# A hybrid attention, SSM and MoE trunk on one core: the layer-1 mixer in another order

## The chip, the cores and the metric

The kernel runs on one core of a Trainium2 chip. The time is the device time of one execution, in microseconds; the median of three runs is given. TensorE does the matmuls, VectorE (DVE) and ScalarE (ACT) the elementwise work, GpSimd (POOL) a little of it, and SyncE (SP) issues the loads of the weights from HBM.

## The reference

A trunk of two layers over 256 tokens of width 1024, all in float32. Layer 0 is sliding-window attention with cross attention to a memory, and a dense SwiGLU. Layer 1, whose first half this change is about, is an SSM mixer and a mixture of eight experts:

```python
z, xbc, dt_raw, xq = split(h @ w_in)                 # 2048, 3072, 32, 1024 columns
xbc = silu(causal_depthwise_conv(xbc, conv_w, conv_b))   # 4 taps
xs, bmat, cmat = split(xbc)                          # 2048, 512, 512
dt = softplus(dt_raw + dt_bias);  a = -exp(a_log)
y = ssd_chunked_scan(xs, dt, a, bmat, cmat)          # 2 chunks of 128, 4 groups of 8 heads of 64
y = y + xs * d_skip
y = rmsnorm(y * silu(z), g_norm)
cross = memory_cross_attention(xq, mem_k, mem_v)     # 4 heads of 256
x = x + concatenate([y, cross]) @ w_out              # (2048 + 1024) x 1024
...
def step(state, inp):                                # one chunk of the scan
    acum = cumsum(dtk * a);  decay = exp(acum[t] - acum[s]) for s <= t
    y_diag = (ck bk^T * decay) @ (xk * dtk)
    y_off = (ck @ state) * exp(acum)
    new_state = state * exp(acum[-1]) + bk^T @ (to_end * xk * dtk)
```

## The kernel before

The program is one instruction list per engine, written out by hand and ordered by semaphores; nothing is scheduled by a compiler. The weights stream through in units of 1 MB: 8 x 128 rows by 256 columns (kind "a") or 4 x 128 rows by 512 columns (kind "b"). A unit is loaded into one of three ring slots, ScalarE writes its high part (`whi`, three buffers, `split_hi`), VectorE the rest (`wlo`, two buffers, `split_lo`), and TensorE multiplies three pairs of high and low parts (`mm3`), so a product keeps about float32 precision. On both engines `ahead(n)` does the splits up to unit n at the place in the list where it stands. The high part of unit n waits until unit n-3 has been used, the low part until unit n-2 has been.

Products of the projections go to four PSUM banks in turn (`PB[f % 4]` for fill f); `drained` counts the banks emptied. Bank 4 and 5 hold scores or transposes, 6 and 7 the rest.

The layer-1 mixer goes through its parts in this order on TensorE (from L1507 on):

1. four units of cross-attention queries, then the scores of head 20 (the four heads are numbered 20 to 23);
2. the small dt unit, and four units of B and C, with transposes, scores and values of a head behind each;
3. eight units of x, each followed by the transposes of the x unit before (`x_transposes`);
4. the scan: eight steps, s = 0 to 7, over two chunks of four groups. A step multiplies B with C (L1560), makes the decay sums of 2 x 4 heads (L1570), the new state (L1577) or the output of the old one (L1582), and the diagonal part for 8 heads (L1589). ScalarE takes the exponential of the decay (L720), VectorE multiplies it by the masked product (L1076), GpSimd makes decay rows (L464), x times dt (L471) and two more products (L477, L481);
5. eight units of z, in two banks per pair, whose silu VectorE multiplies into y (L1098); ScalarE sums the squares;
6. rstd of y on GpSimd (L442 to L448), y scaled on VectorE (L860), 32 transposes in groups of four pairs with high and low part behind each (L1298, L533, L869);
7. twelve units of the output projection, six per 512 columns, y first and cross attention last, and the addition to x.

The causal conv of a unit (`for j in range(12)` on ScalarE and VectorE) copies the fill from PSUM into `ub`, which has three columns of zeros ahead (L687). For each of its two tiles VectorE multiplies by the last tap and adds the bias (L1048), adds the other three taps one after the other (L1052), and ScalarE applies silu (L696):

```python
ve.tensor_scalar(cv[:, k, :], u[:, CW - 1:], w[:, CW - 1:CW], ..., ALU.mult, ALU.add)
for tap in range(CW - 2, -1, -1):
    ve.scalar_tensor_tensor(out=cv[:, k, :], in0=u[:, tap:tap + S], scalar=w[:, tap:tap + 1], in1=cv[:, k, :], ...)
```

Of the kernel before, what the change touches and what calls it, by code (L numbers as in the profile page):

```python
# [21 lines left out]
P = 128  # L22
# [72 lines left out]
def weight_units(a):  # L95
# [64 lines left out]
def trunk(nc, a, out):  # L160
    units = weight_units(a)
    XQ0, K0, V0, OUT0, K1, FFN0 = 5, 9, 13, 17, 25, 29
    V1, L1, MOE = FFN0 + 3 * FC, FFN0 + 3 * FC + 4, len(units)

    ctx = ExitStack()
    with ctx:
# [11 lines left out]
        cat_hi, cat_lo = sb("cat_hi", [P, 24, S], F32R), sb("cat_lo", [P, 24, S], F32R)  # L178
# [39 lines left out]
        with ExitStack() as l1:  # L218
            with ExitStack() as conv:
                ub = sb("ub", [P, 2, 2, S + CW - 1], F32, conv)  # L220
                cv = sb("cv", [P, 2, S], F32, conv)
                xcT = sb("xcT", [P, 2, 2, S], F32, conv)
            with ExitStack() as scan:
                zs = sb("zs", [P, 2, 512], F32, scan)
# [3 lines left out]
            sb("pair_d", [P, 2600], F32, l1)  # L228
            dtx, dtu, dtr_, dtm, dt, dta = (sb(n, [P, NT, NH], F32, l1) for n in ("dtx", "dtu", "dtr", "dtm", "dt", "dta"))
            cbm = sb("cbm", [P, P], F32, l1)  # L230
            btok = sb("btok", [P, P], F32, l1)
            xdt = sb("xdt", [P, HPG, PH], F32, l1)
        with ExitStack() as moe:
# [10 lines left out]
        sb("pair_e", [P, 2 * 2 * S + NT * 2 * 192 + NT * D])  # L244
        Lm = actf[:, :, :].rearrange("p a (h t) -> p a h t", h=4)
# [24 lines left out]

        hankel = [c[:, 16:24, :] for c in (cat_hi, cat_lo)]
# [10 lines left out]
            dt_ready ln_chain dta_full eac_done u_zero conv_chain conv_done silu_conv xT_full xs_ready hi_ready lo_ready  # L282
# [3 lines left out]
            yd_full yo_full yo_done yy_done yg_done rt_chain rt_exp final""".split()  # L286
# [41 lines left out]
        TR_BEFORE = {R_H0: 0, R_MEM0: 4, R_MEM1: 8, R_F0: 12, R_H1: 16, R_Y: 20, R_F1: 28}  # L328
        XN_BEFORE = {R_H0: 0, R_MEM0: 2, R_F0: 4, R_H1: 6, R_Y: 8, R_F1: 10, R_FIN: 12}
# [3 lines left out]
        def square_at(r, t, n):  # L333

            if r in (R_H0, R_MEM0):
                return SQ_BEFORE[r] + t
            return SQ_BEFORE[r] + (2 * t + n if r in (R_H1, R_FIN) else 2 * n + t)

        fills, last_unit = {}, []
        for name, start, n, per in (("kv", 0, 1, 1), ("q", 1, 4, 1), ("xq0", XQ0, 4, 1), ("k0", K0, 4, 1), ("v0", V0, 4, 2),  # L340
                                    ("out0", OUT0 + 6, 4, 1), ("k1", K1, 4, 1), ("v1", V1, 4, 2), ("xq1", L1, 4, 1), ("dt", L1 + 4, 1, 1),
                                    ("bc", L1 + 5, 4, 1), ("x", L1 + 9, 8, 1), ("z", L1 + 17, 8, 2), ("out1", L1 + 25, 4, 6)):
# [145 lines left out]
        def _(ac):  # L488
# [180 lines left out]
            for j in range(4):  # L669
                xq_out("xq1", j)  # L670
# [1116 lines left out]
```

## Time and profile before

| | us |
|---|---|
| median of 3 runs | 1677.37 (1677.33 to 1680.08) |
| profiled execution, its time | 1680.51 |
| profiled execution, its span | 1678.7 |
| TensorE busy | 1561.9 (93%) |
| VectorE busy | 1122.6 (67%) |
| ScalarE busy | 951.7 (57%) |
| GpSimd busy | 64.2 (4%) |
| mean granted clock of TensorE | 0.959 |

The span runs from the first to the last instruction of the core. Busy time is the time in which an engine had an instruction under way. The granted clock is a share of the full speed: 1.00 is 2.4 GHz, 0.50 is 1.2 GHz. A busy share averages over stages that have different limits, so the rows below are cut by stage: the mixer of layer 1 runs from 460.4 to 807.2 us.

### The profile page before, as it was taken

The page shows a single profiled execution, that of the slowest core. Times are in us where ns is not written, and L with a number is a line of the kernel's source. Part 1 is how long each engine was busy: PE and PEld are TensorE (multiplying, and loading weights), DVE is VectorE, ACT ScalarE, POOL GpSimd, SP SyncE. Part 2 cuts the span into 40 slices and gives each one's busy share as a digit, 9 for nine tenths or more (in the row PEclk, how much of TensorE's full clock was granted, in tenths as well). Part 3 has the DMA queues.
Part 4 walks back from the last instruction along what each step waited for, and adds up shares of the span by engine and source line. Part 5 has one row for each costly group of instructions (what it writes and reads, how often), then busy time and mean ns, then how long its engine had stood idle before and what let it go on. Part 6 is the DMA issues. An engine that isn't in the chain of part 4 may idle for free.

```text
span 1678.7 us, 22515 instructions
## 1 busy us (share of the span) xinstructions
PE 1561.9 (93%) x8652; PEld 1357.4 (81%) x8652; DVE 1122.6 (67%) x997; ACT 951.7 (57%) x959; POOL 64.2 (4%) x85
## 2 busy tenths in 40 slices
PE   6999999999998768969599999999999999999996
PEld 6998899999897757858478788888888888888885
DVE  4455454444646655444498788797978978788885
ACT  5444453434546432433356777777677776777763
POOL 1000000000100026000000000000000000000000
PEclk9999999999999979979689999999999999999998
DMA  8433355656543420425479999999998999989992
GB/s 268 150 102 126 124 177 178 197 178 191 181 134 101 126 76 1 151 75 176 150 253 344 324 326 373 319 350 332 332 371 310 349 341 333 355 314 365 328 346 111
DMA packets 229602, 391.88 MB, mean 233 GB/s; under 512 B 7280, under 2 KB 82208, under 8 KB 229536
## 3 DMA queue, kind: packets, MB, share of 16 engines
q1 hardware_dynamic: 229536, 390.96, 67.2%
q8 instruction: 46, 0.75, 0.2%
q14 instruction: 20, 0.16, 0.0%
HBM read 389.86 MB, written 1.07 MB: 233 GB/s over the span
## 4 chain that ended last, share of the span: by engine, by line
PE 74%; DVE 8%; DMA 6%; issue 5%; ACT 5%; POOL 0%; SPq 0%; ACTq 0%; DVEq 0%; POOLq 0%
PE PB L1279 22%; PE PB L1280 21%; PE PB L1281 21%; DMA y<-in_moe_w_down 4%; DVE cv L1052 2%; ACT whi L496 1%; PE PB L1642 1%; DVE xn_lo L847 1%; PE PB L1619 1%; DMA ring<-in_moe_w_gate 1%; PE PB L1298 1%; PE PB L1570 1%; ACT whi L501 1%; ACT hT_hi L501 1%; PE PB L1361 1%
## 5 line engine op out<-in xcount | busy, mean ns | idle before, releaser
L1279 PE MATMUL PB<-whi,cat_hi 128*128 128x512 f32 (+1 forms) x1048 | 405.9, 387 | 14.4 <-DVE cat_lo L1229 11.5
L501 ACT ACTIVATE whi<-ring 128x2048 fp32r<-128x2048 f32 x168 | 321.0, 1916 | 142.6 <-PE PB L1281 118.2
L1281 PE MATMUL PB<-whi,cat_lo 128*128 128x512 f32 (+1 forms) x1048 | 399.1, 381 | 0.0
L841 DVE TENSOR_TENSOR wlo<-ring,whi 128x2048 fp32r<-128x2048 f32 (+1 forms) x103 | 234.1, 2273 | 205.4 <-PE PB L1281 171.4
L1280 PE MATMUL PB<-wlo,cat_hi 128*128 128x512 f32 (+1 forms) x824 | 309.0, 375 | 0.0
L847 DVE TENSOR_TENSOR wlo<-ring,whi 128x2048 fp32r<-128x2048 f32 x112 | 255.5, 2288 | 66.8 <-ACT whi L501 66.7
L1279 PEld LDWEIGHTS PB<-whi,cat_hi 128*128 128x128 f32 x1048 | 200.2, 191 | 51.5 <-DVE wlo L847 11.3
L1281 PEld LDWEIGHTS PB<-whi,cat_lo 128*128 128x128 f32 x1048 | 199.9, 191 | 37.7
L496 ACT ACTIVATE whi<-ring 128x2048 fp32r<-128x2048 f32 (+1 forms) x103 | 195.4, 1899 | 52.2 <-PE PB L1281 41.3
L1279 PE MATMUL PB<-hT_hi,whi 128*128 128x256 f32 x744 | 215.8, 290 | 2.7 <-DVE hT_lo L869 1.8
L1280 PE MATMUL PB<-hT_lo,whi 128*128 128x256 f32 x744 | 212.9, 286 | 0.0
L1281 PE MATMUL PB<-hT_hi,wlo 128*128 128x256 f32 x744 | 212.8, 286 | 0.0
L1280 PEld LDWEIGHTS PB<-wlo,cat_hi 128*128 128x128 f32 x824 | 156.4, 190 | 26.2
L1279 PEld LDWEIGHTS PB<-hT_hi,whi 128*128 128x128 f32 x744 | 145.6, 196 | 3.8 <-DVE hT_lo L869 2.2
L847 DVE TENSOR_TENSOR hT_lo<-ring,whi 128x2048 fp32r<-128x2048 f32 x56 | 128.2, 2288 | 28.9 <-ACT whi L501 28.9
L1280 PEld LDWEIGHTS PB<-hT_lo,whi 128*128 128x128 f32 x744 | 145.4, 195 | 0.5
L1281 PEld LDWEIGHTS PB<-hT_hi,wlo 128*128 128x128 f32 x744 | 145.1, 195 | 0.0
L847 DVE TENSOR_TENSOR elo<-y,hT_hi 128x2048 fp32r<-128x2048 f32 x56 | 128.2, 2289 | 16.5 <-ACT hT_hi L501 16.1
L501 ACT ACTIVATE hT_hi<-y 128x2048 fp32r<-128x2048 f32 x56 | 107.4, 1918 | 37.2 <-PE PB L1281 31.0
L847 DVE TENSOR_TENSOR xn_lo<-y,st_hi 128x2048 fp32r<-128x2048 f32 x40 | 91.5, 2288 | 10.9 <-ACT st_hi L501 10.9
L1280 PE MATMUL PB<-hT_lo,cat_hi 128*128 128x512 f32 x224 | 90.2, 403 | 0.0
L1279 PE MATMUL PB<-hT_hi,cat_hi 128*128 128x512 f32 x224 | 88.7, 396 | 0.0
(248 smaller groups left out, 2215.1 us busy)
## 6 DMA issues: line engine op xcount, KB each, us to landing
ring<-in_moe_w_gate SPq DMA_DIRECT2D x64, 1024.0 KB, 6.8
ring<-in_moe_w_up SPq DMA_DIRECT2D x64, 1024.0 KB, 7.4
y<-in_moe_w_down SPq DMA_DIRECT2D x48, 1024.0 KB, 8.0
ring<-in_moe_w_down SPq DMA_DIRECT2D x40, 1024.0 KB, 5.7
ring<-in_ssm_w_in SPq DMA_DIRECT2D x24, 1024.0 KB, 5.3
y<-in_moe_w_up SPq DMA_DIRECT2D x24, 1024.0 KB, 8.1
y<-in_moe_w_gate SPq DMA_DIRECT2D x24, 1024.0 KB, 6.8
ring<-in_w_mem_kv SPq DMA_DIRECT2D x16, 1024.0 KB, 5.4
```

What stands on the lines that cost most here:

```text
L496: nc.scalar.activation(whi[:, n % HIS, 0:w], ring[:, n % RING, 0:w], ACT.Copy).then_inc(q["hi_ready"], 1)
L501: nc.scalar.activation(ehi[slot(m)], eraw[slot(m)], ACT.Copy).then_inc(q["hi_ready"], 1)
L841: ve.tensor_tensor(wlo[:, n % LOS, 0:w], ring[:, n % RING, 0:w], whi[:, n % HIS, 0:w].bitcast(F32), ALU.subtract).then_inc(q["lo_ready"], 1)
L847: ve.tensor_tensor(elo[slot(m)], eraw[slot(m)], ehi[slot(m)].bitcast(F32), ALU.subtract).then_inc(q["lo_ready"], 1)
L1052: i = ve.scalar_tensor_tensor(out=cv[:, k, :], in0=u[:, tap:tap + S], scalar=w[:, tap:tap + 1], in1=cv[:, k, :], op0=ALU.mult, op1=ALU.add)
L1279: mm(out, lhs[0], rhs[0], start=start, stop=False)
L1280: mm(out, lhs[0], rhs[1], start=False, stop=False)
L1281: return mm(out, lhs[1], rhs[0], start=False, stop=stop)
L1298: last = nc.tensor.transpose(PB[4 + f % 2][:, S * i + P * t:S * i + P * t + P], src[:, t, P * (2 * g + i):P * (2 * g + i) + P], ident)
L1361: last = mm(bank[:, S * j:S * j + S], xqT[:, 2 * h + k, P * j:P * j + P], memK[:, 2 * h + k, :], start=k == 0, stop=k == 1)
L1570: last = mm(PB[4 + n % 2][:, P * h:P * h + P], Lm[:, n % 2, h, :], tri, start=True, stop=True)
L1619: last = mm(PB[GATHER_BANK[i]][:, P * k:P * k + P], src[:, t, P * (4 * (i % 2) + k):P * (4 * (i % 2) + k) + P], sel[:, t, :], start=t == 0 ...
```

## The change

Only the mixer of layer 1 and the order of its weights are changed.

- **Attention.** Scores, transposes and values of the four heads are set between the units from the second query unit on.
- **Conv.** ScalarE makes the first tap with its bias straight from PSUM into the destination (`BCT`, or `xcT`, now four buffers deep). VectorE adds the other three taps, also straight from PSUM, in place, the two tiles in turn; the columns on the left that a tap doesn't reach are left out, so `ub` and its zeros go. Silu is applied in place, a unit at a time for x, in two pieces for all of B and C.
- **z between x.** The weights come as two x units, two z units, and so on. Silu of z goes into a buffer of its own, `zsilu`. B is transposed for all groups at once, ahead of the scan.
- **Scan in half steps.** n = 0 to 15. TensorE issues the decay sums of the next half step ahead of this one's diagonal part, and in each half step a quarter of a unit of the cross projection (`cross_quarter`), whose four units have been moved to the front of the output projection. B times C is made a step ahead, into two buffers of `cbm`. The diagonal part uses one bank and `xdt` has two buffers. The gate (times silu of z) follows each step, and the transposes, high and low parts of the finished 512 columns of y follow one or two steps later (`y_turn`, `y_hi_step`, `y_lo_step`).
- **rstd of y on the rows.** y is transposed without being scaled; its product with the weights collects in four banks of its own, and `rstd` is applied as it is added to x.

```diff
-    units += [(cols(w, DI + 256 * j, 256), "a") for j in range(8)]
-    units += [(kb(w, kg, n), "b") for n in range(4) for kg in range(2)]
-    units += [(kb(a["ssm_w_out"][0], kg, n), "b") for n in range(2) for kg in range(6)]
+    for n in range(4):
+        units += [(cols(w, DI + 256 * j, 256), "a") for j in (2 * n, 2 * n + 1)]
+        units += [(kb(w, kg, n), "b") for kg in range(2)]
+    units += [(kb(a["ssm_w_out"][0], kg, n), "b") for n in range(2) for kg in (4, 5)]
+    units += [(kb(a["ssm_w_out"][0], kg, n), "b") for kg in range(4) for n in range(2)]
...
# GpSimd, a step of the scan
+                if s >= 2:
+                    pool.wait_ge(q["yd_full"], 2 * (s - 1))
+                pool.tensor_tensor(xdt[s % 2][:, :, :], xs, dt[:, c, HPG * g:HPG * g + HPG]...).then_inc(q["xdt_ready"], 1)
...
+                if s + 1 < 2 * G:
+                    decay_rows(2 * s + 2)
                 if s >= 1:
-                    pool.wait_ge(q["yy_done"], s)
+                    pool.wait_ge(q["yd_drained"], s)
...
+                if s + 1 < 2 * G:
+                    decay_rows(2 * s + 3)
...
# ScalarE, conv and z
+            def conv_in(j):
+                f = conv_fill(j)
+                ahead(last_unit[f] + 2)
+                fill_ready(ac, f)
...
+                    last = nc.scalar.activation(dst, PB[f % 4][:, S * k:S * k + S], ACT.Identity, scale=pc[:, w:w + 1],
+                                                bias=pc[:, PC_CB + tile:PC_CB + tile + 1])
+                last.then_inc(q["cv_ready"], 1)
...
+            for n in range(4):
+                conv_in(4 + 2 * n)
...
+                conv_in(5 + 2 * n)
...
+                silu_x(2 * n)
+                ahead(XZ + 4 * n + 4)
+                silu_x(2 * n + 1)
+                xs_copy(2 * n)
...
+                for t in range(NT):
+                    gemm_out(z_fill(n, t), y_tiles(zsilu, t, n), func=ACT.Silu)
...
# ScalarE, scan
+            decay_exp(0)
+            decay_exp(1)
             for s in range(2 * G):
                 c, g = divmod(s, G)
...
+                if s + 1 < 2 * G:
+                    decay_exp(2 * s + 2)
+                if s >= 2:
+                    y_hi_step(s - 2)
+                ahead(CROSS1 + s // 2 + 2)
+                if s >= 1:
+                    y_square(s - 1)
+                if s + 1 < 2 * G:
+                    decay_exp(2 * s + 3)
...
# VectorE, conv and scan
+                for tap in range(CW - 2, -1, -1):
+                    lag = CW - 1 - tap
+                    for k in range(2):
...
+                        i = ve.scalar_tensor_tensor(out=cv, in0=PB[f % 4][:, S * k:S * k + S - lag], scalar=pc[:, w:w + 1], in1=cv,
+                                                    op0=ALU.mult, op1=ALU.add)
...
+                m_step(2 * s + 1)
+                if s >= 2:
+                    y_lo_step(s - 2)
+                if s in (2, 4, 6):
+                    ahead(CROSS1 + s // 2 + 1)
+                if s + 1 < 2 * G:
+                    cb_mask(s + 1)
+                    m_step(2 * s + 2)
+                if s == G - 1:
+                    for t in range(NT):
+                        cross_add(0, t)
...
+                ve.tensor_tensor(x4, x4, y_tiles(zsilu, c, g), ALU.mult).then_inc(q["yg_done"], 1)
+            y_lo_step(6)
+            for t in range(NT):
+                cross_add(1, t)
+            ahead(YOUT + 2)
+            y_lo_step(7)
+            ahead(MOE - 1)
...
+                    ve.scalar_tensor_tensor(out=xv, in0=PB[4 * n + t][:, :], scalar=rstd[:, c:c + 1], in1=xv,
+                                            op0=ALU.mult, op1=ALU.add).then_inc(q["y_added"], 1)
...
# TensorE, scan and output
+            for n in range(4 * G):
+                s, half = divmod(n, 2)
+                if half and s + 1 < 2 * G:
+                    scan_cb(s + 1)
+                if n + 1 < 4 * G:
+                    scan_seg(n + 1)
+                cross_quarter(n)
+                if half == 0:
+                    scan_state(s)
+                scan_yd(n)
+                if half and s >= 1:
+                    y_turn(s - 1)
+            for kg in range(4):
+                for n in range(2):
...
+                    if kg == 0:
+                        if n == 0:
+                            pe.wait_ge(q["cross_done"], 4)
...
+                    if kg == 0 and n == 0:
+                        y_turn(2 * G - 1)
```

## Rows read from the trace of the kernel before

**Rows 1.** The page: the chain that ended last, share of the span by engine

```profile
PE 74%; DVE 8%; DMA 6%; issue 5%; ACT 5%; POOL 0%; SPq 0%; ACTq 0%; DVEq 0%; POOLq 0%
```

**Rows 2.** Windows; stretch: length, busy of PE PEld DVE ACT POOL, PEclk, DMA, GB/s

```profile
460.90:537.00 76.10, 69.92 (x511) 67.19 (x511) 41.78 (x64) 41.12 (x58) 2.04 (x2) 0.96 0.39 119
537.00:614.20 77.20, 55.98 (x420) 53.78 (x419) 51.78 (x83) 30.69 (x45) 0.00 (x0) 0.89 0.39 123
614.20:671.20 57.00, 46.63 (x292) 39.48 (x292) 30.02 (x40) 16.56 (x29) 39.27 (x34) 0.88 0.00 1
671.20:716.60 45.40, 45.35 (x192) 37.14 (x192) 19.66 (x13) 20.95 (x24) 0.79 (x3) 0.96 0.45 149
716.60:738.90 22.30, 7.97 (x33) 5.87 (x32) 13.01 (x21) 11.55 (x25) 3.59 (x7) 0.58 0.21 75
738.90:807.50 68.60, 68.20 (x288) 55.59 (x288) 25.02 (x14) 19.23 (x15) 1.30 (x4) 0.96 0.46 160
```

**Rows 3.** Timeline of TensorE: start, us, engine, line, operation (queries, scores, dt)

```profile
460.36 0.28 PE L1279 MATMUL PB<-hT_hi,whi 128*128 128x256 f32 x1
...
466.11 0.28 PE L1279 MATMUL PB<-hT_hi,whi 128*128 128x256 f32 x1
...
484.44 1.97 PE L1361 MATMUL PB<-memK,xqT 128*128 128x256 f32 x8 [0.89 <-ACT xqT L540]
486.05 0.37 PE L1279 MATMUL PB<-whi,hT_hi 128*128 128x32 f32 x1
...
491.69 0.56 PE L1279 MATMUL PB<-hT_hi,whi 128*128 128x256 f32 x1
```

**Rows 4.** Timeline of VectorE in the output projection: two splits in a row

```profile
747.11 2.29 DVE L841 TENSOR_TENSOR wlo<-ring,whi 128x2048 fp32r<-128x2048 f32 x1 [8.23 <-PE PB L1281]
752.55 2.29 DVE L841 TENSOR_TENSOR wlo<-ring,whi 128x2048 fp32r<-128x2048 f32 x1 [3.15 <-PE PB L1281]
```

**Rows 5.** Timeline of VectorE in the x units: two splits in a row

```profile
552.89 2.29 DVE L841 TENSOR_TENSOR wlo<-ring,whi 128x2048 fp32r<-128x2048 f32 x1 [1.11 <-ACT whi L496]
...
561.72 2.29 DVE L841 TENSOR_TENSOR wlo<-ring,whi 128x2048 fp32r<-128x2048 f32 x1 [2.77 <-ACT whi L496]
```

**Rows 6.** Instructions of lines L869 and L533: duration ns min/median/max, first and last start

```profile
L869 DVE SCALAR_TENSOR_TENSOR cat_lo<-PB,pc,cat_hi x32: 473/476/485, 31.3 to 738.4; 128x256 fp32r<-128x256 f32 x32
L533 ACT ACTIVATE cat_hi<-PB,pc x32: 467/474/493, 30.4 to 737.5; 128x256 fp32r<-128x256 f32 x32
```

**Rows 7.** Timeline of TensorE in the scan

```profile
617.88 3.46 PE L1570 MATMUL PB<-con,actf 128*128 128x128 f32 x16
...
644.44 0.44 PE L1560 MATMUL PB<-BCT 128*128 128x128 f32 x2
644.71 1.95 PE L1570 MATMUL PB<-con,actf 128*128 128x128 f32 x16
646.50 1.02 PE L1582 MATMUL PB<-st,BCT 128*128 128x512 f32 x2
647.42 1.08 PE L1589 MATMUL PB<-xdt,nt 128*128 128x64 f32 x8
```

**Rows 8.** Groups of instructions from 614 to 671 us: busy us, mean ns | idle before

```profile
L720 ACT ACTIVATE nt<-PB 128x512 f32<-128x512 f32 x16 | 9.6, 597 | 36.5 <-PE PB L1570 36.2
L1089 DVE TENSOR_TENSOR y<-y,yo 128x512 f32<-128x512 f32 x4 | 2.8, 693 | 0.1
L1070 DVE TENSOR_TENSOR cbm<-PB,con 128x128 f32<-128x128 f32 x8 | 2.3, 285 | 5.3 <-PE PB L1560 5.3
L496 ACT ACTIVATE whi<-ring 128x2048 fp32r<-128x2048 f32 x1 | 1.9, 1902 | 0.0
L710 ACT ACT_TABLE_LOAD x1 | 1.3, 1283 | 0.0
```

**Rows 9.** Instructions of lines L1076 and L464: duration ns min/median/max

```profile
L1076 DVE TENSOR_TENSOR nt<-nt,cbm x16: 692/1002/1522, 620.5 to 667.0; 128x512 f32<-128x512 f32 x16
L464 POOL TENSOR_TENSOR actf<-con,dta x16: 1041/1482/1488, 498.3 to 660.9; 128x512 f32<-128x512 f32 x16
```

More of the change, by code:

```diff
@@ new lines, in y_hi_step @@
+            def y_hi_step(s):
+                c, g = divmod(s, G)
+                ac.wait_ge(q["tr_full"], TR_BEFORE[R_Y] + s + 1)
+                ac.wait_ge(q["sq_done"], square_at(R_Y, c, g) + 1)
+                for i in range(4):
+                    k = 4 * g + i
+                    last = nc.scalar.activation(cat_hi[:, k, P * c:P * c + P], PB[3][:, P * i:P * i + P], ACT.Identity, scale=pc[:, PC_GN + k:PC_GN + k + 1])
+                last.then_inc(q["t_hi"], 1)
+            decay_exp(0)
@@ L1101, in _ @@
[L1101 to L1104 removed]
+                                     eac[:, HPG * g:HPG * g + HPG].unsqueeze(2).to_broadcast([P, HPG, PH]), ALU.mult).then_inc(q["yo_read"], 1)
+                    ve.wait_ge(q["yo_read"], s - G + 1)
+                    ve.tensor_tensor(xs, xs, yo[:, :], ALU.add).then_inc(q["yo_done"], 1)
+                    ve.wait_ge(q["yo_done"], s - G + 1)
@@ new lines, in scan_yd @@
+            def scan_yd(n):
+                s = n // 2
+                if n % 2 == 0:
+                    pe.wait_ge(q["xdt_ready"], s + 1)
+                    if s == 0:
+                        bank_drained(pe, 2)
+                    else:
+                        pe.wait_ge(q["yd_drained"], s)
+                pe.wait_ge(q["m_ready"], n + 1)
+                for h in range(4):
+                    hh = 4 * (n % 2) + h
+                    last = mm(PB[2][:, PH * hh:PH * hh + PH], dec[:, n % 2, h, :], xdt[s % 2][:, hh, :], start=True, stop=True)
+                last.then_inc(q["yd_full"], 1)
@@ new lines, in cross_quarter @@
+            def cross_quarter(i):
+                n, kg, t, half = i // 8, i // 4 % 2, i // 2 % 2, i % 2
+                u = CROSS1 + i // 4
+                w = parts(u, "b")
+                split_ready(u)
+                if kg == 0 and half == 0:
+                    if n == 0:
+                        bank_drained(pe, t)
+                    else:
+                        pe.wait_ge(q["cross_done"], t + 1)
+                for k in (2 * half, 2 * half + 1):
+                    last = mm3(PB[t][:, :], cut(cat, ALL, 16 + 4 * kg + k, slice(P * t, P * t + P)), cut(w, ALL, k), kg == 0 and k == 0, kg == 1 and k == 3)
+                if half == 1 and t == 1:
+                    last.then_inc(q["units_used"], 1)
+                if half == 1 and t == 0 and kg == 1:
+                    last.then_inc(q["cross_full"], 1)
@@ new lines, in y_turn @@
+            def y_turn(s):
+                c, g = divmod(s, G)
+                pe.wait_ge(q["yg_done"], s + 1)
+                if s == 0:
+                    bank_drained(pe, 3)
+                else:
+                    pe.wait_ge(q["t_lo"], TR_BEFORE[R_Y] + s)
+                for i in range(4):
+                    last = nc.tensor.transpose(PB[3][:, P * i:P * i + P], y[:, c, 512 * g + P * i:512 * g + P * i + P], ident)
+                last.then_inc(q["tr_full"], 1)
+            scan_cb(0)
```

481 lines of the change are left out of this document (269 added, 212 removed).

## The prediction

> **What bounds the kernel now.** I read the chain of work that ended last first: nearly three quarters of it is TensorE [rows 1]. So what this change can give is time in which TensorE waits, or runs at its lower clock. The windows then cut the layer-1 mixer, from the first matmul of its cross-attention queries (460.4 us) to the last of its output projection (807.2 us), into six stretches [rows 2]: queries, attention, dt and B/C units (75.3 us, to 535.7); x units (78.5); scan (57.0); z units (45.4); the gap with the norm of y (22.3); output projection (68.3). They add up to 346.8 us. In the z and output stretches TensorE is busy all the time. In the x stretch it is busy 56 of 77 us, in the scan 47 of 57, in the gap 8 of 22, and its granted clock falls to 0.88 in the first two and 0.58 in the last. These are the places to win back.
>
> What TensorE needs when nothing holds it back comes from its timeline. A 256-column unit ("a") goes from 460.36 to the next unit's start at 466.11: 5.75 us. A 512-column unit ("b") is paced 5.44 us, read off the starts of two successive splits. Scores of a head take 1.61 us (484.44 to 486.05), dt 5.64 (486.05 to 491.69) [rows 3, 4]. I take values at 1.61 too, since they are eight matmuls of the same size, and four transposes at 0.44, a quarter of the 16 decay matmuls of the same size, 1.79 from 644.71 to 646.50 [rows 7].
>
> **Part 1, attention and B/C.** The change only spreads the four heads between units. TensorE's floor is 8 x 5.75 + 5.64 + 4 x (1.61 + 1.61 + 0.44) = 66.3 us. I walked the three queues through it: each head's max, exponential and division fall under the next unit. The latest of them, the last head's division, comes some 49 us in, and its transposes are wanted at about 53. The narrow matmuls of dt leave the lower clock behind them, as now (0.96 mean over this stretch [rows 2]), so I add 1 us: 67.4. Gain 7.9.
>
> **Part 2, x units with z between.** Today each x unit is a round through three engines. DVE splits the next weights, does 2 x 4 dependent taps, ScalarE applies silu, copies the transposed x, and only then makes the next high part, for which DVE waits 2.77 us; the round is 8.83 us (552.89 to 561.72) for 5.75 us of matmuls [rows 5]. The change takes the first tap off DVE, drops the copy out of PSUM, and puts two z units, which need no taps, behind each pair. DVE per group of four units: 12 taps at 0.476, which the same operation on PSUM takes [rows 6], plus four splits of 2.29, some 15 us. ScalarE per group: four splits of 1.9, four first taps at 0.474 [rows 6], two silus, two copies and two evacuations of 0.6 each [rows 8], some 13 us. TensorE needs 2 x 5.75 + 2 x 5.44 + 2 x 0.44 = 23.3. Both others have room, and walked through, every split lands 2 to 4 us before its unit is wanted; the first group has two table loads and the big silus of B/C, 4 us more on ScalarE, still inside. The first taps are thus costed at nothing because they lie beside matmuls; without that cover they would be 24 x 0.474 = 11 us. The first-tap write is Identity into xcT, four buffers deep now, so no wait on the transposes. Sum: 4 x 23.3, the two small matmuls for the decay (0.4) and four B transposes (0.4), 0.5 for clock: 94.5, against 78.5 + 45.4 = 123.9. Gain 29.4.
>
> **Part 3, the scan.** A step now costs TensorE: product of B and C 0.27 (644.44 to 644.71), decay matmuls 1.79, state or its output 0.92, the diagonal part twice eight pieces at 1.0 [rows 7]; new inside it are two quarters of the cross projection, 2 x 6 matmuls at 5.44/24, 2.72, and four transposes of y, 0.44. That is 8.14 us a step, 64.7 for eight with seven turns. What goes on top:
> - Start: after the last z unit ScalarE does two evacuations, one copy, one split, a table load of 1.28 [rows 8] and the exponential before VectorE can multiply; TensorE has only about 5 us of work for the 6.4. 1.4 us.
> - In steps 2, 4 and 6 VectorE has a weight split of 2.29 between the low part of y and the next half step's multiplication, and the high part of y, on ScalarE, waits behind an exponential. From the end of the decay matmuls: exponential 0.7, high part 1.1, low part 1.2 (four narrow pieces; between the 0.285 of a 128 x 128 product [rows 8] and 0.476 each [rows 6], nearer the first), split 2.3, mask 0.3, multiplication 1.0: 6.6 us, where TensorE has 5.5 to 6 to do. 3 x 1.2 = 3.6.
> - The two cross additions in step 3: 1.0.
> - GpSimd. Its decay rows take 1.04 us at their shortest and 1.48 at the median, and VectorE's multiplication 0.69 and 1.00 [rows 9]: they slow each other. VectorE now has the gate and the split beside GpSimd too. Between 0 and the 4.2 to 5.2 us that GpSimd works in a step, I take 0.6 a step, 4.8, as most lies in slack.
> Scan: 64.7 + 1.4 + 3.6 + 1.0 + 4.8 = 75.5, against 57.0: 18.5 dearer, but 21.8 of it is cross projection that leaves the last stretch.
>
> The Trainium skill, "SBUF — State Buffer", section "SBUF: two separate sides", says the pair of ports is locked for a whole instruction and the loser fully blocks, also for a VectorE instruction with two SBUF inputs against a GpSimd one that reads SBUF. By that rule in full the scan would come to what rival B gives. The rows fit it so far: the longest multiplication took 1.52 [rows 9], which is under the 1.73 of one that first waits out a whole decay row. But they can't tell a full block from a part of one.
>
> The Trainium skill, "ScalarE: Activation LUTs", section "Terms", puts a table load at about 2.7 us; by it the start of the scan would be 1.4 us dearer. The row says 1.28, and it decides.
>
> **Part 4, from the scan to the rows of the output.** The gap of 22.3 us goes: no row scaling of y, no burst of transposes with both engines behind each, since the sum of squares is only needed on the output rows. A new wait takes part of its place: the first output unit needs banks 0 and 1, which VectorE empties behind the last gate. After the last diagonal matmuls VectorE does three operations and the gate, 0.69 each [rows 8] (3.0 with handoffs), the low part of y (1.2) and two additions (1.4): 5.7 us. Queued behind them is the split of the second unit, ready long before it is wanted. Then eight units x 5.44 = 43.5, one turn 0.5, and after such an idle stretch the lower clock, about 2 us (the output stretch now has 68.3 for 65.3 of matmuls; the z stretch 45.4 for 43.5 [rows 2]). Sum 51.7, against 22.3 + 68.3 = 90.6: gain 38.9. The last addition, with rstd, is one operation on the same shape as now, so what follows 807.2 is as it was. Weights come in the same number and pieces; the DMA share was under half in all six stretches [rows 2], three units ahead.
>
> **Sum.** 67.4 + 94.5 + 75.5 + 51.7 = 289.1 against 346.8: 57.7 us less. The profiled execution spans 1678.7 and took 1680.5; it would be 1621.0 and 1622.8. The median of the runs is 3.1 below the profiled time, so 1677.4 - 57.7 = 1619.7; I say 1619.5.
>
> **Rivals.**
> - A, as above: 1610 to 1630 with the unknown costs. Chance 0.62.
> - B, VectorE becomes the bound of the scan. Its own work in a late step is 2 x 0.69 + 0.3 + 4 x 0.69 + 1.2 + half a split 1.15 = 6.8, with handoffs some 7.3, and GpSimd's 4.2 (four operations of 1.04) is added in full: 11.5 a step, 92 instead of 75.5: 1636. For it: the slowed multiplications; against it: most of what GpSimd does can run while VectorE reads PSUM or waits. 0.17.
> - C, the conv still runs through its three-engine round at 8.83 us a unit: 8 x 3.1 = 25 more, 1644. For it: the same three engines are still in the round, in strict order. Against it: silu and first tap now work on different units, and there are z units to catch up in. This is the rival in which the reordering doesn't do what it says. 0.08.
> - D, the other side: TensorE's lower clock. Sixteen decay pieces took 3.46 us at the lower clock (617.88) and 1.95 at the upper one (644.71) [rows 7]; a scan wholly at the lower costs 1.5 for these and, where the rest doubles at most, 2.4 (cross) + 0.9 (state) + 0.3 (product) + 1.0 (half of the diagonal's 2.0) + 0.4 (turn) = 6.5 a step, 52 us, which takes nearly the whole gain (1671). It becomes slower than before when the lower clock also holds over two of the output units (5.4 more for each); over all eight it would be 1715. For it: the scan now shows 0.88, narrow matmuls and waits. Against it: with 2.7 us of wide matmuls in each step, TensorE is busier than in any part of today's scan. 0.03, of which 0.02 slower than now.
> - E, everything hides: no contention, stalls or clock loss, 289.1 - 13 = 276: 1606.5. 0.10.
>
> **How the numbers follow.** The prediction is A's. The range runs from E's end to just past B, 1606 to 1638; C and D, 0.11, are left out, and a little at E's edge. A measurement of this kernel can tell about 0.2% (3.4 us). Faster takes A, B, C, E and a part of D: 0.97; same 0.01; slower 0.02.
>
> **What would show it.** The profile after should show: no idle of TensorE over 1 us between x and z units and a clock near 1.00 there (part 2); steps of 8 to 9.5 us in the scan, with waits on VectorE's multiplication in the steps with a split (part 3); one idle of about 5 us before the output units and a short lower clock behind it (part 4). The forecast is wrong if steps reach 11 us, if x units wait for their weights' low part, or if the clock in the scan falls under 0.9.

## The result, and the profile after

The changed kernel takes 1625.35 us (median of 4 runs, 1617.28 to 1627.27) against 1677.35 (1676.79 to 1680.08): ratio 0.968, 95% interval 0.965 to 0.971. Run again in a later series (e1 below), it had a median of 1619.86. The forecast was 1619.5, with a range of 1606 to 1638.

The page gives the chain that ended last, share of the span by engine; its TensorE share has gone from 74% [rows 1] to 80%:

```profile
PE 80%; DMA 6%; DVE 6%; issue 4%; ACT 4%; SPq 0%; POOL 0%; DVEq 0%; ACTq 0%; POOLq 0%
```

In the changed kernel's trace the first query matmul, with which the mixer begins, starts at 461.11 us (before: 460.36). Its windows, cut at the new borders: queries, attention, dt and B/C; x and z units; scan; exit from the scan; output projection to its last matmul. Columns as in [rows 2]:

```profile
461.11:530.90 69.79, 69.79 (x512) 67.91 (x511) 37.01 (x57) 32.66 (x50) 4.10 (x2) 0.95 0.43 131
530.90:625.35 94.45, 94.45 (x620) 86.31 (x619) 57.90 (x71) 55.16 (x63) 0.00 (x0) 1.00 0.56 177
625.35:700.35 75.00, 65.99 (x414) 55.65 (x412) 50.66 (x75) 32.16 (x66) 45.89 (x41) 0.98 0.20 60
700.35:705.40 5.05, 0.16 (x2) 0.01 (x1) 4.95 (x11) 3.47 (x7) 1.15 (x4) 0.93 0.00 0
705.40:752.40 47.00, 46.98 (x196) 38.40 (x196) 19.11 (x14) 12.99 (x16) 1.07 (x3) 0.94 0.46 164
```

Set against [rows 2], each stretch has lost what the change aimed at. TensorE is now busy in every microsecond of the first two, 164.24 in all. The x units had 56 of 77. In the scan it is busy 66 of 75, and the gap with the norm of y has shrunk to 5. The mixer takes 291.3 us (461.1 to 752.4) instead of 346.8, 55.5 less. The profiled span fell by more, 63.3, because the code behind the mixer, which nobody touched, took 862.8 instead of 871.5 in this execution. In the scan and at its exit TensorE's waits are few enough to list. The chain of waits of the changed kernel, 625 to 700 us (who waited for what: us in total, times, longest):

```profile
PE PB L1775 <- DVE cat_lo L1179: 3.8, 5, 0.8
PE PB L1733 <- DVE yo L1213: 3.1, 2, 1.5
PE PB L1746 <- DVE nt L1171: 1.5, 1, 1.5
PE PB L1728 <- POOL xde L513: 0.6, 1, 0.6
```

and TensorE's timeline at the exit:

```profile
705.42 0.77 PE L1413 MATMUL PB<-whi,cat_hi 128*128 128x512 f32 x1 [4.90 <-DVE x L1189]
705.98 0.63 PE L1414 MATMUL PB<-wlo,cat_hi 128*128 128x512 f32 x1
...
711.98 0.39 PE L1414 MATMUL PB<-wlo,cat_hi 128*128 128x512 f32 x1
```

Thus 9.0 us of waits in the scan, 4.9 behind it, and after that some 6 us in which 512-column matmuls start 0.43 apart instead of 0.23: the lower clock. The wait on the multiplication (L1171) occurs once, at the start. The forecast expected it in three later steps.

### The profile page after: what moved, and what is told of

Its sections match the earlier page's. It is cut to its first block, busy times and chain, and to the rows that moved or that the text cites. A ratio compares the mean times of both kernels' runs of the same rounds, so it can differ in the third digit from the quotient of the medians.

```text
span 1615.4 us, 22522 instructions
## 1 busy us (share of the span) xinstructions
PE 1540.5 (95%) x8652; PEld 1342.5 (83%) x8652; DVE 1110.5 (69%) x990; ACT 946.2 (59%) x963; POOL 69.6 (4%) x85
## 4 chain that ended last, share of the span: by engine, by line
PE 80%; DMA 6%; DVE 6%; issue 4%; ACT 4%; SPq 0%; POOL 0%; DVEq 0%; ACTq 0%; POOLq 0%
PE PB L1413 23%; PE PB L1414 23%; PE PB L1415 23%; DMA y<-in_moe_w_down 4%; DMA ring<-in_moe_w_gate 2%; PE PB L1858 1%; PE PB L1835 1%; DVE xn_lo L929 1%; ACT whi L541 1%; PE PB L1495 1%; PE PB L1526 1%; ACT hT_hi L541 1%; PE PB L1719 1%; PE PB L1520 1%; PE PB L1432 1%
## 5 line engine op out<-in xcount | busy, mean ns | idle before, releaser
L1413 PEld LDWEIGHTS PB<-whi,cat_hi 128*128 128x128 f32 x1048 | 199.7, 191 | 51.3 <-DVE wlo L929 9.6
L929 DVE TENSOR_TENSOR elo<-y,hT_hi 128x2048 fp32r<-128x2048 f32 x56 | 128.2, 2289 | 15.9 <-ACT hT_hi L541 15.4
```

The costliest lines, as they stand in the source:

```text
L929: ve.tensor_tensor(elo[slot(m)], eraw[slot(m)], ehi[slot(m)].bitcast(F32), ALU.subtract).then_inc(q["lo_ready"], 1)
L1413: mm(out, lhs[0], rhs[0], start=start, stop=False)
```

## The experiments

Each of the kernels e1 to e12 was profiled once and timed in five rounds, the changed one in a series of its own; the kernel before, timed beside them in three series, had medians of 1676.49, 1676.46 and 1677.37. "Scan" runs from the first product of B and C to the start of the last diagonal matmul, "exit and output" from there to the start of the last addition of y, "rest" from there to the end of the span. "Mixer" runs from the first query matmul, which starts between 459.5 and 461.3 us, to the start of that addition, 0.2 us behind the last matmul in the changed kernel. All four are of the profiled execution and good to 0.1 us (before: mixer 346.8 and rest 871.5, cut at the last matmul).

| kernel | median (range) | ratio to before, 95% | scan | exit and output | mixer | rest |
|---|---|---|---|---|---|---|
| changed | 1625.35 (1617.28 to 1627.27) | 0.968 (0.965 to 0.971) | 74.4 | 52.8 | 291.5 | 862.8 |
| e1, the same again | 1619.86 (1613.26 to 1622.48) | 0.966 (0.964 to 0.968) | 74.4 | 52.8 | 291.4 | 865.2 |
| e2, cross projection after the scan | 1626.81 (1624.53 to 1634.19) | 0.971 (0.969 to 0.974) | 65.8 | 71.3 | 301.4 | 861.9 |
| e3, GpSimd's scan rows narrow | 1621.24 (1617.79 to 1625.58) | 0.968 (0.965 to 0.970) | 74.4 | 51.3 | 291.6 | 867.9 |
| e4, other column half first | 1610.47 (1605.70 to 1615.52) | 0.961 (0.959 to 0.963) | 72.8 | 45.8 | 283.0 | 862.1 |
| e5, high part of y first | 1610.03 (1604.40 to 1613.53) | 0.960 (0.957 to 0.963) | 65.4 | 51.6 | 281.3 | 861.3 |
| e6, dt in two halves | 1617.20 (1615.52 to 1622.50) | 0.964 (0.961 to 0.967) | 78.7 | 51.9 | 291.8 | 868.3 |
| e7, x units, then z | 1635.70 (1629.27 to 1642.84) | 0.974 (0.971 to 0.977) | 72.2 | 52.8 | 308.6 | 871.4 |
| e8, first tap on VectorE | 1620.60 (1612.72 to 1627.41) | 0.965 (0.962 to 0.968) | 78.7 | 51.9 | 294.9 | 870.3 |
| e9, e4 and e5 | 1605.26 (1596.11 to 1609.65) | 0.957 (0.954 to 0.959) | 67.0 | 45.9 | 277.1 | 861.3 |
| e10, e4, e5 and e6 | 1602.27 (1594.41 to 1610.45) | 0.954 (0.952 to 0.957) | 68.6 | 45.8 | 275.5 | 872.7 |
| e11, e7 with the copy first | 1620.28 (1617.03 to 1625.76) | 0.967 (0.965 to 0.969) | 73.7 | 51.5 | 289.6 | 867.7 |
| e12, e10 and exponentials first | 1600.06 (1596.66 to 1605.29) | 0.954 (0.952 to 0.956) | 63.7 | 45.9 | 273.8 | 864.3 |

### e1: the same kernel again

No edit.

> The changed kernel unaltered. Its first profiled execution spans 1615.4 us, while four others of it took 1624.6 to 1627.3, so its trace is of an unusually short one. The mixer of layer 1 took 292.0 us in it (460.4 to 752.4) and what follows 863.0 us, against 871.5 in the trace of before. Theory 1: the mixer always takes about 292 us and the part behind it, untouched by the change, varies from execution to execution; then this trace, if it spans about 1624, shows the mixer within 1 us of 292.0 and the rest near 871. Theory 2: the mixer varies (its clock or its handoffs fall out otherwise); then the mixer is near 300 here and the rest near 863. Median expected 1620 to 1627.

The mixer takes 291.4 us, as in the first profile (291.5), with the same waits to 0.1 us. The two executions differ behind the mixer: 862.8 and 865.2 here, 861.3 to 872.7 over all kernels, in code that no edit touches. So the stages compare to about 1 us where the clock is the same, and medians of different kernels only to some 5 us.

### e2: the cross projection after the scan

```diff
-                cross_quarter(n)
...
+            for n in range(4 * G):
+                cross_quarter(n)
```
with its splits and additions moved behind the scan as well.

> The sixteen quarters of the cross projection, with their splits and additions, go behind the scan; all else stays. Theory 1 (the quarters fill time in which TensorE would wait for the other engines): the scan without them falls from 75.0 us only to about 58 to 62, the cross projection costs its 21.8 us behind it and the exit wait gets a little shorter, so the mixer is 5 to 10 us longer and the time about 7 us above the changed kernel. Theory 2 (TensorE is already full in the scan): the scan falls by the whole 21.8, to 53, and the time is unchanged within 2 us. Theory 3 (the wide matmuls hold up the clock): the granted clock in the scan falls from 0.98 to under 0.92 and the loss is over 10 us.

Of 21.8 us of matmuls taken out of the scan, only 8.6 came off it. The windows of this kernel, scan first, then the cross units:

```profile
625.50:691.30 65.80, 49.91 (x313) 41.88 (x312) 43.23 (x69) 26.83 (x63) 44.44 (x38) 0.87 0.06 20
691.30:713.50 22.20, 19.04 (x87) 15.48 (x87) 11.13 (x14) 7.08 (x9) 2.32 (x7) 1.00 0.30 95
```

and the waits in its scan:

```profile
PE PB L1773 <- DVE cat_lo L1178: 9.7, 5, 2.1
PE PB L1726 <- POOL xde L513: 2.9, 2, 2.0
PE PB L1731 <- DVE yo L1207: 1.7, 3, 0.7
PE PB L1744 <- DVE nt L1170: 1.5, 3, 0.6
```

Waits are 15.8 us instead of 9.0, and the clock is 0.87 instead of 0.98. So with the quarters in the scan 6.8 us of waits are filled, and most of the rest goes with the higher clock. Whether it is their width that holds the clock up, or that fewer waits are left, this run can't tell. Their place is worth 9.9 us of the mixer (301.4 against 291.4) and 7.0 of the median.

### e3: GpSimd's rows in the scan narrow

```diff
-   pool.tensor_tensor(Lm[:, n % 2], su.unsqueeze(1).to_broadcast([P, 4, P]), ...)
+   w = P if n < 4 else 8
+   pool.tensor_tensor(Lm[:, n % 2, :, 0:w], su[:, 0:w].unsqueeze(1).to_broadcast([P, 4, w]), ...)
```
and in the same way for its three products of x. This kernel leaves out most columns of the decay rows and of these products from the third step on.

> From the third step of the scan on, GpSimd computes only a narrow part of its rows (8 of 128 columns of the decay rows, 4 of 64 of the others), so these products are stale for the most part; every instruction, wait and buffer stays. This takes most of GpSimd's port time away. Theory 1 (contention costs the scan about 0.6 us a step, the rest is slack): the scan gets 2 to 5 us shorter. Theory 2 (GpSimd's time is the bound through VectorE): 10 us or more. Theory 3 (contention lies wholly in slack; the steps are paced by the order of waits): under 1 us, while VectorE's multiplications still fall from about 1.0 to 0.7 us each.

The multiplication on VectorE, which [rows 9] show for the kernel before: duration ns min/median/max, first in the changed kernel, then here:

```profile
L1171 DVE TENSOR_TENSOR nt<-nt,cbm x16: 684/914/1546, 630.5 to 697.3; 128x512 f32<-128x512 f32 x16
```

```profile
L1173 DVE TENSOR_TENSOR nt<-nt,cbm x16: 684/693/1544, 630.5 to 697.1; 128x512 f32<-128x512 f32 x16
```

GpSimd does slow the multiplication: the median falls from 914 to 693 ns once GpSimd's operations from the third step on take 0.24 us alone instead of 1.04 (the two multiplications at the start, beside full rows, stay at 1.5). But the scan takes 74.4 us, as in e1, and TensorE's four waits have the same numbers. So from the third step on the contention lies wholly in slack. That disproves the forecast's 0.6 a step there, and rival B. At the start, which this run left as it was, the contention is on the path: the first multiplication lasts 1.55 instead of 0.69 us and TensorE waits 1.5 for it, so some 0.9 of that wait is GpSimd's (an estimate from these rows, not run).

The forecast left open whether one engine blocks the other in full or in part. Starts and lengths settle it. In the changed kernel:

```profile
657.86 0.69 DVE L1220 TENSOR_TENSOR y<-y,zsilu 128x512 f32<-128x512 f32 x1
...
657.90 1.55 POOL L519 TENSOR_TENSOR xsD<-y,pr 128x512 f32<-128x512 f32 x1 [5.23 <-DVE y L1209]
...
658.47 1.53 DVE L1171 TENSOR_TENSOR nt<-nt,cbm 128x512 f32<-128x512 f32 x1
...
659.41 1.48 POOL L495 TENSOR_TENSOR actf<-con,dta 128x512 f32<-128x512 f32 x1
```

Suppose that the one that starts first keeps its own length (0.69 us on VectorE, 1.04 on GpSimd), and that the other waits until about 0.55 or 0.90 us of it are over and then takes its own length. That gives 1.55, 1.53 and 1.48 here, and it gives the length of each of the 59 such operations from 628 to 700 us (VectorE's with two inputs from SBUF, and GpSimd's) to within 0.01 us; 30 of them were lengthened. In e3 a GpSimd operation of 0.24 us still took 0.75 beside the gate. An operation of VectorE that reads PSUM (`yo`, 0.69 at 675.74) and GpSimd's beside it (1.05 at 675.79) kept their lengths. So it is a full block, for nearly the whole of the other's instruction, and this trace agrees with the rule of the Trainium skill ("SBUF — State Buffer", "SBUF: two separate sides") that whichever instruction starts first gets the shared pair of ports for the whole of it and the other fully blocks. What failed is the step from there to rival B's 92 us: it added all of GpSimd's time to VectorE's, where only operations that meet wait, and VectorE, busy 50.7 of 75 us, had slack for them.

### e4: the other column half first at the exit

```diff
-    units += [(kb(a["ssm_w_out"][0], kg, n), "b") for kg in range(4) for n in range(2)]
+    units += [(kb(a["ssm_w_out"][0], kg, n), "b") for kg in range(4) for n in ((1, 0) if kg == 0 else (0, 1))]
...
-            y_lo_step(6)
             for t in range(NT):
                 cross_add(1, t)
-            ahead(YOUT + 2)
+            ahead(YOUT + 1)
+            y_lo_step(6)
+            ahead(YOUT + 2)
```
The first output unit now goes to banks 4 and 5, free since the last exponential; the last turn of y stands behind the second unit.

> The first output unit is the one that collects in banks 4 and 5, not the one that needs banks 0 and 1; VectorE does the two last cross additions and one more split ahead of the low part of y, and the last turn of y comes after two units. Theory 1 (the 4.9 us idle behind the scan is the wait for banks 0 and 1, and the lower clock behind it costs about 2.5 us more): the stretch from the end of the scan to the end of the output falls from 52.0 to 45 to 47 us, the time by 5 to 7 us. Theory 2 (another wait stands right behind: the gates, or the split of the second unit): under 2 us is won.

Exit and output fall by 7.0 us, to 45.8, and the idle of 4.90 becomes one of 0.49, on the unit's low part:

```profile
PE PB L1414 <- DVE wlo L923: 0.5, 1, 0.5
```

The windows of scan and output show a clock of 1.00 (0.94 in the output stretch of the changed kernel):

```profile
624.50:697.30 72.80, 63.81 (x409) 53.62 (x408) 50.37 (x74) 32.11 (x66) 45.89 (x40) 1.00 0.18 62
697.30:743.00 45.70, 45.20 (x203) 36.66 (x202) 24.24 (x24) 16.36 (x22) 4.67 (x9) 1.00 0.48 169
```

So 4.4 of the 7.0 was the wait for the banks and most of the rest the clock behind it. The 1.6 in the scan is the clock too (1.00 instead of 0.98), for its waits are unchanged: such a stretch differs between executions, as "What stays open" below says.

### e5: the high part of y ahead of the exponential

```diff
-                if s + 1 < 2 * G:
-                    decay_exp(2 * s + 2)
                 if s >= 2:
                     y_hi_step(s - 2)
+                if s + 1 < 2 * G:
+                    decay_exp(2 * s + 2)
```

> One swap on ScalarE: the high part of the finished y of step s-2 comes ahead of the exponential of half step 2s+2. In the changed kernel TensorE waits for VectorE in the scan in five turns of y (3.8 us) and two products of the state (3.1 us), and the chain there reads exponential, high part, low part, split. Theory 1 (the high part stands too late in ScalarE's order and delays all that follows on VectorE): the five waits of the turns go, the two on the state shrink, the scan falls from 74.4 us to 67 to 71. Theory 2 (VectorE is simply full in these steps): the scan stays within 1 us of 74.4.

Why the turns waited is in the timeline of the changed kernel, one of the five places:

```profile
651.30 0.60 ACT L785 ACTIVATE nt<-PB 128x512 f32<-128x512 f32 x1 [1.41 <-PE PB L1719]
...
651.80 1.14 ACT L800 ACTIVATE cat_hi<-PB,pc 128x128 fp32r<-128x128 f32 x4
...
652.97 1.13 DVE L1179 SCALAR_TENSOR_TENSOR cat_lo<-PB,pc,cat_hi 128x128 fp32r<-128x128 f32 x4 [4.32 <-ACT cat_hi L800]
...
654.01 2.28 DVE L923 TENSOR_TENSOR wlo<-ring,whi 128x2048 fp32r<-128x2048 f32 x1
...
654.24 0.63 PE L1775 MATMUL PB<-con,y 128*128 128x128 f32 x4 [0.76 <-DVE cat_lo L1179]
```

The high part stands behind an exponential that waits for decay matmuls, though its own input has long been there; the low part waits for the high part; bank 3 is free only then, and the next turn of y needs that bank. VectorE's split comes behind the low part, and everything after it is late too. With the two lines swapped the waits in the scan are

```profile
PE PB L1746 <- DVE nt L1171: 1.5, 1, 1.5
PE PB L1728 <- POOL xde L513: 0.6, 1, 0.6
PE PB L1733 <- DVE yo L1213: 0.6, 1, 0.6
```

The turns' waits are gone, 3.1 on `yo` has become 0.6, and the scan takes 65.4: 9.1 us less for 6.3 us of waits. Of the rest 1.6 goes with the clock, 1.00 here, for that is what the scan of e4 had less at the same clock with its waits unchanged; what is left, 1.2, no view names. The median falls by 9.8 against e1.

### e6: the dt unit in two halves

```diff
             for t in range(NT):
                 for k in range(KD):
                     last = mm3(PB[f % 4][:, NH * t:NH * t + NH], ...)
+                if t == 0:
+                    gemm_a_fill(L1 + 5, fills["bc"], hT, (0,))
             last.then_inc(q["units_used"], 1)
-            gemm_a_fill(L1 + 5, fills["bc"], hT)
+            gemm_a_fill(L1 + 5, fills["bc"], hT, (1,))
```

> The 48 narrow matmuls of dt are no longer in a row: the second 24 come after the first half of the next unit. In the changed kernel the granted clock falls to 0.5 near the end of dt and stays there for 6.8 us, 3.3 us lost, and the stretch up to the x units takes 70.5 us. Theory 1 (a long row of narrow matmuls lets the clock fall): the clock stays at 1.00 and the stretch falls to 67 to 68. Theory 2 (the fall has another cause, or 24 in a row are enough): the stretch stays at 70 to 71, or the fall only moves.

One window in each kernel, 496 to 504 us, the changed one first. TensorE has no gap in either:

```profile
496.00:504.00 8.00, 8.00 (x43) 8.00 (x44) 2.85 (x4) 1.91 (x1) 0.00 (x0) 0.57 0.29 81
```

```profile
496.00:504.00 8.00, 8.00 (x65) 7.83 (x64) 4.05 (x5) 2.94 (x3) 0.00 (x0) 1.00 0.08 16
```

TensorE's timeline of the changed kernel shows the step, from 0.11 to 0.22 us a matmul, near the end of the row of 48 matmuls of 32 columns:

```profile
496.18 0.26 PE L1413 MATMUL PB<-whi,hT_hi 128*128 128x32 f32 x1
496.29 0.26 PE L1414 MATMUL PB<-wlo,hT_hi 128*128 128x32 f32 x1
...
497.44 0.37 PE L1414 MATMUL PB<-wlo,hT_hi 128*128 128x32 f32 x1
497.66 0.37 PE L1415 MATMUL PB<-whi,hT_lo 128*128 128x32 f32 x1
```

With 24 and 24 the clock stayed up here, and the decay's small matmuls come 72.8 us behind the first query matmul instead of 75.9. All ten profiles of changed kernels with 48 in a row show the lower clock in this place (0.53 to 0.70 from 496 to 504 us), and of the three with 24 and 24 the one of e12 does too, behind each half (0.86 and 0.72 in two windows of 8 us; its small matmuls come at 75.8). So the long row is the likely cause, but shorter ones don't rule the fall out. The profiled scan of e6 took 78.7 with the same kinds of waits (8.5 us in all), for its clock was 0.91. So the mixer of that execution shows nothing of the gain, and the median is 2.7 below e1's, with intervals that overlap.

### e7 and e11: all x units, then all z units

e7 puts the eight x units ahead of the eight z units again. Its order on ScalarE was

```diff
+            for j in range(8):
+                conv_in(4 + j)
...
+                if j >= 1:
+                    silu_x(j - 1)
+                if j >= 3:
+                    xs_copy(j - 3)
```

> Conv as changed, but all eight x units first and then all eight z units, as before the change. Between the first x unit and the scan the changed kernel takes 94.4 us. Theory 1 (what counts is the shorter conv and that the silu no longer stands ahead of the split; VectorE needs 5.0 us per x unit against 6.2 of TensorE): the stretch stays within 1.5 us of 94.4. Theory 2 (the z units between are what gives the other engines time to catch up): x units take 7 us or more each and the stretch grows by 6 us or more.

x and z together took 113.8 us (530.9 to 644.7) instead of 94.4. The chain in order of time shows one round, and the waits from 531 to 645 what held TensorE:

```profile
565.80 0.35 issue
566.15 0.55 ACT xcT L720
566.70 0.52 ACT xcT L726
567.22 0.49 ACT y L623
567.72 0.14 issue
567.85 0.89 PE PB L1684 x4
```

```profile
PE PB L1684 <- ACT y L623: 11.0, 5, 2.2
```

Each round is 10.1 us, and it hangs on a copy: the transposes of x (L1684) need the bank that the copy (L623) empties, and I had put that copy behind the first tap of a later unit, which waits for that unit's matmuls. The waits are 11.0 of the 19 us lost; behind each the 256-column matmuls start 0.21 us apart instead of 0.12, and the clock of the stretch is 0.92. That is an order of mine, not of the change; so e11 moves the copy ahead of the first tap, and nothing else:

```diff
             for j in range(8):
+                if j >= 3:
+                    xs_copy(j - 3)
                 conv_in(4 + j)
...
-                if j >= 3:
-                    xs_copy(j - 3)
```

> All x units, then all z units, as in the earlier run of that kind, but with ScalarE's copy of the transposed x ahead of the first tap of the next unit, so that the transposes no longer wait for it. Theory 1: what that earlier run lost was mostly its own order on ScalarE; x and z units together come near 94.4 + 3, and the place of the z units buys next to nothing: the gain of the stretch came from the taps. Theory 2: the place of the z units matters: without them the x units run at the pace of the round through three engines, 8 us or more each, and the stretch stays at 108 to 114 us. In between, each us over 94.4 is what the z units' place gives.

```profile
531.00:560.00 29.00, 29.00 (x245) 29.00 (x245) 23.17 (x35) 21.39 (x26) 0.00 (x0) 1.00 0.53 157
560.00:590.00 30.00, 29.88 (x217) 28.05 (x217) 20.45 (x29) 18.39 (x24) 0.00 (x0) 1.00 0.50 167
590.00:621.00 31.00, 31.00 (x141) 25.63 (x140) 12.53 (x7) 14.05 (x14) 2.65 (x2) 1.00 0.60 196
```

In the first window, all of it x units, VectorE is busy 23.2 of 29 us and TensorE always. The scan starts at 625.5, as in the changed kernel (625.4), and the median is 1620.28 against e1's 1619.86. So with the changed conv z between x gives nothing. The gain of this stretch must then come from the conv or from the order of the queues (first tap on ScalarE, no copy to `ub`, silu and splits in another order); which of these carries it was not separated. e7's loss, 19.0 us of the mixer against e11 and 15.4 of the median, was one copy at the wrong place in one queue.

### e8: the first tap on VectorE

```diff
-                    last = nc.scalar.activation(dst, PB[f % 4][:, S * k:S * k + S], ACT.Identity, ...)
+                    last = ve.tensor_scalar(dst, PB[f % 4][:, S * k:S * k + S], ..., ALU.mult, ALU.add)
```

> The first tap of the conv goes back to VectorE (still from PSUM), all else as changed: 24 x 0.41 us more on VectorE, 24 x 0.47 less on ScalarE. Theory 1 (with z between x both engines have room): the stretch from the first x unit to the scan stays within 1 us of 94.4, the time within noise of the changed kernel. Theory 2 (taking the tap off VectorE carries part of the gain): 3 us or more slower.

With z between x it costs this stretch nothing: the scan starts at 624.5, TensorE is busy all the time. VectorE's work in the stretch grows from 57.9 to 66.3 us of 94, still under TensorE's. The tap's move and the place of z are each dispensable while the other is there; both undone at once was not run.

### e9, e10 and e12: what helps, together

e9 joins e4 and e5, e10 adds e6. e12 also puts ScalarE's split of a later cross unit behind the first two exponentials:

```diff
-            ahead(CROSS1 + 2)
...
             decay_exp(0)
             decay_exp(1)
+            ahead(CROSS1 + 2)
```

> The changed kernel with both edits that helped by themselves: the first output unit in the banks of the cross projection's second column half (and the last turn of y behind the second unit), and the high part of y ahead of the exponential. Theory 1: they stand at different places (exit wait, turns in the scan) and add up: mixer near 282 less 9, 272 us, and about 1601 us as median. Theory 2: they share a resource, VectorE's late queue: with the turns' waits gone VectorE runs closer behind TensorE, so the exit wait was already shorter, and together they give hardly more than one: mixer 278 to 281, median 1607 to 1610.

> As the run before, and the second half of the B units' first matmuls between the two halves of dt as well. Theory 1: the 3 us that the lower clock behind dt's narrow matmuls cost come off the stretch before the x units (534 instead of 537 for the decay's small matmuls), mixer near 269, median about 1598. Theory 2: the clock falls elsewhere instead and the mixer stays where the run before has it, within 1 us.

> As the run with all three edits, and ScalarE's split of a later cross unit behind the first two exponentials of the scan instead of ahead of them. Theory 1: the wait of the first diagonal matmuls on the multiplication (1.5 us) and the lower clock of 629 to 637 us behind it (0.79 or 0.6) come from that split; both shrink, mixer 2 to 4 us less. Theory 2: GpSimd's first operations, beside which both multiplications take 1.5 us each, set the start too; the wait falls by 1 us at most and the mixer by as little.

e9 keeps both effects in the waits, but its mixer (277.1) lies between what full addition (273) and none (281) would give: it has 67.0 in the scan, at a clock of 0.97, where e5 had 65.4 at 1.00. In e10 the small matmuls come 3.1 us earlier than in e9 (72.8 against 75.9 behind the first query matmul), and half of that is given back by a scan at a lower clock. In e12 the wait on the multiplication is gone, and its scan is the shortest:

```profile
PE PB L1736 <- DVE yo L1213: 0.7, 2, 0.6
PE PB L1731 <- POOL xde L513: 0.6, 1, 0.6
PE PB L1414 <- DVE wlo L923: 0.5, 1, 0.5
```

```profile
624.00:687.70 63.70, 62.31 (x409) 53.33 (x408) 53.12 (x74) 32.09 (x66) 48.08 (x40) 1.00 0.21 71
```

So the split was what the start waited for, although both first multiplications still run beside GpSimd. e12 has the lowest median, 1600.06: 1.2% under e1, with intervals far apart. Between e10 and e12 the ratios (0.9544 and 0.9543) show no difference.

## Why the prediction was right, and where it was not

- **Part 1, 67.4 forecast, 69.8 measured.** The step that failed is "so I add 1 us" for the lower clock behind dt. It cost about 3.3: some 7 us at the lower level, half speed (0.57 over 8 us). The other terms held to 0.2 in sum (69.8 - 3.3 = 66.5 against 66.3): six of the eight scores and values took 1.73 instead of 1.61, and transposes 0.36 instead of 0.44.
- **Part 2, 94.5 forecast, 94.4 measured.** The sum held, clock 1.00, no idle. But the reason was half wrong: the z units behind each pair, in rival C "z units to catch up in", were to let the splits be in time. e11 shows that the x units keep TensorE's pace without them. (The 11 us for uncovered first taps count 24 taps; 16 of them lie in this stretch.)
- **Part 3, 75.5 forecast, 75.0 measured: right by luck, with errors that cancel.** Too high: 4.8 for GpSimd, which from the third step on was nothing (e3); 1.0 for the cross additions, behind which no wait is listed; and the matmuls, costed at 64.7. Those took some 63.0: in e12 the scan takes 63.7 with 1.3 of waits, and the last diagonal matmul and the turn behind it add 0.6; half of a diagonal part takes 0.83 to 0.92 us, not 1.0. That is 7.5 too much. Too low: the waits, 9.0 instead of 1.4 and 3.6, and 3.0 that were not in the sum at all, of which 1.7 is the clock (0.79 from 629 to 637 us) and 1.3 stays unexplained. That is 7.0 too little. The mechanism of the 3.6 was half right. The chain (exponential, high part, low part, split) is the one forecast, but TensorE never waited at its end, the multiplication. It waited for what the low part releases, bank 3: the turns of y waited 3.8 us in five steps, also in those without a split. And in the step behind two of the three splits the state's output waited 1.54 for `yo`. The working followed the chain to what VectorE does next and never asked who waits for the bank that the low part empties. Start: 1.4 forecast, 1.5 and 0.6 measured.
- **Part 4, 51.7 forecast, 52.0 measured.** The wait was 4.9 instead of 5.7 and stood where forecast, on the banks (e4). The lower clock cost nearer 2.8 than 2: 14 matmuls at 0.43 instead of 0.23.
- **Sum.** 289.1 forecast, 291.3 measured; the miss is part 1. The forecast also held that what follows the mixer is as it was. In the profiles it took 871.5 before and 861.3 to 872.7 after, with the same code, and the medians of one kernel lie 5.5 us apart (1625.35 and 1619.86, forecast 1619.5). So a hit within 1 us, or a miss of 6, is chance; what the profiles bear out is the 55.5 us of the mixer.
- **Rivals.** B falls with e3. C did not come, but e7 shows that it was possible: one copy at another place in ScalarE's queue brings a round of 10.1 us. D did not come, but e2 (0.87 in the scan without the cross matmuls) shows what helped to hold it off. E did not come with this kernel; e12's mixer, 273.8, lies under E's 276.

What stays open: the same scan, with waits between 8.5 and 9.0 us, took 72.2 and 72.8 us in two executions at a clock of 1.00 (e7, e4), 73.7 to 74.4 in four at 0.98 (changed, e1, e3, e11), and 78.7 in two at 0.91 (e6, e8). In e12, dt in halves stood at 0.86 and 0.72 from 488 to 504, where e6 and e10 had 1.00. What tips the clock between such executions was not found. And what in part 2 gives the gain of 29.4 us is known only by exclusion: the place of z and the tap's move are each dispensable while the other is there.

## What to carry over

When an operation is moved behind another in an engine's queue, follow its chain to every resource that it releases, above all the PSUM bank, and not only to the next instruction of the same engine: two swapped lines gave 9.8 us, and one misplaced copy cost 19. A first consumer should be given the bank that has been free longest, not the one emptied last. And before work on an engine is counted as the price of a step, ask whether it lies in slack: from the third step on a multiplication a third longer cost nothing.

## What the runs showed of the hardware

- TensorE's granted clock can fall without any gap in its work: near the end of 48 matmuls of 32 columns that started 0.11 us apart it went to its lower level for about 7 us (0.57 in that window), so that the 256-column matmuls that followed started 0.21 apart instead of 0.12. With the row cut into 24 and 24 it stayed at 1.00 in two of three profiles and fell behind each half in the third.
- A scan filled with 512-column matmuls ran at a clock of 0.98, without them at 0.87, so 21.8 us of added matmuls lengthened it by 8.6.
- A GpSimd operation of 1.04 us and a VectorE operation of 0.69 with two inputs from SBUF block each other. The one that started first kept its length, and the other waited until all but its last 0.14 us was over. In a row of them both therefore took up to 1.55 us, and in e5 a GpSimd operation that met a weight split took 2.90. Beside a VectorE operation that reads PSUM neither was lengthened.
